# RWKV scan with partition halves holding the two scan directions of one head: 128-row products and fused score products

## The chip, the cores and the metric

The kernel runs on one core of one Trainium2 chip. The metric is the device time of one launch in microseconds (us); the change is judged by the median of several runs. Engines are named as in the profile: PE is TensorE (matrix products), PEld its weight loads, DVE is VectorE, ACT is ScalarE, POOL is GpSimd, SP is SyncE, which here only issues transfers.

## The reference

One encoder layer on a prompt of 256 tokens and a sample of 1024 tokens: feed-forward half step, token mixing, cross attention, feed-forward half step, each followed by a layer norm. Token mixing runs two groups side by side: gated linear attention, and RWKV-7 with 8 heads of 64 channels in both directions of time. The change touches only the RWKV recurrence, which the reference writes as:

```python
def _rwkv7_scan(r, decay, k, v, kk, a, reverse):
    def step(S, inp):
        r_t, w_t, k_t, v_t, kk_t, a_t = inp
        sa = jnp.einsum('bhij,bhj->bhi', S, -kk_t)
        S = (S * w_t[:, :, None, :] + sa[..., None] * (kk_t * a_t)[:, :, None, :]
             + v_t[..., None] * k_t[:, :, None, :])
        y = jnp.einsum('bhij,bhj->bhi', S, r_t)
        return S, y
...
y = (_rwkv7_scan(rH, dec_f, k2, vH, kk, aH, reverse=False)
     + _rwkv7_scan(rH, dec_b, k2, vH, kk, aH, reverse=True))
```

All of it is float32. The kernel does it in chunks of C = 64 tokens: 20 chunks (4 of the prompt, 16 of the sample), each in both directions, so a chunk step works on 8 heads x 2 directions = 16 little problems of 64x64 matrices.

## The kernel before

The program is a row of phases with all engines meeting between them. `rwkv_scan_phase` (L1202) is the one that changes; it is written out in full for each chunk, with no loop on the chip, so every product is its own instructions.

Its work is a software pipeline in four stages, `steps` calls `step(n, m, p, s)` for 23 values of n, with m = n+1, p = n+2, s = n+3:

- s: `exponentials` on ACT (L1637, L1638: `rws_grown`, `rws_decayed`) turn the loaded log decays (`rws_pack`) into factors, then `scale` on POOL (L1313 to L1322) multiplies them into `rws_bk` (the terms b and k), `rws_ar` (the terms a and r) and `rws_carry`.
- p: `scores` on PE multiply `bk` by `ar`; DVE masks the results (`mask_with`, L1721) into `rws_gb` and `rws_gk`; `rows` on PE transpose `bk` through an identity and ACT copies that out (L1673).
- m: a triangular system is inverted by doubling, in five levels: `lower`, a mask on DVE (`mask_lower`, L1715, `rws_y`), `extend`, and the copies `take_x` (L1656) and `take_z` (L1666) on ACT.
- n: the state. `rhs_of_v`, `rhs_of_h` and `solve` give `rws_u` (copied by ACT at L1650, once a chunk), `h_of_v` and `h_of_u` the next state, `out_of_h`, `out_of_v`, `out_of_u` the output; DVE adds (L1726, L1736, L1745).

In this layout a partition half `own(e)` (rows 0 to 63 or 64 to 127) holds head e of a pair of heads; direction d and pair q lie along the free axis. Every PE product is one call of `product` (L1343) over 64 rows into 64 columns. Products that alternate e stand in the two halves of the array, and most loops interleave two kinds of product that use different quarters, such as `lower` with `h_of_u`.

Each engine takes its instructions strictly in the order of the text of `step`; semaphores join them. Two waits matter below: `pe.wait_ge(bk_set, ...)` and `pe.wait_ge(ar_set, ...)` hold the first scores of chunk p until POOL has scaled it, and `exponentials` stands at a fixed place in ACT's order.

SP loads, for each chunk, two transfers of `pack` (L1302) and two of `v` (L1303).

Of the kernel before, what the change touches and what calls it, by code (L numbers as in the profile page):

```python
# [20 lines left out]
P = 128  # L21
# [1180 lines left out]
def rwkv_scan_phase(nc, pack_d, out, consts):  # L1202
# [8 lines left out]

    with ExitStack() as ctx:
        m_ = Memory(nc, ctx, "rws")
        slots = lambda name, shape, count: [m_.sb(f"{name}{u}", shape) for u in range(count)]
        BOTH, PAIR, EDGED = [P, 2, 4, C], [P, 2, 4, 2, C], [P, 2, 4, C + 1]
        pack, v = slots("pack", [P, 2, 4, PACK - R_COL], 2), slots("v", BOTH, 4)
        decayed, grown, carry = m_.sb("decayed", EDGED), slots("grown", EDGED, 2), slots("carry", [P, 2, 4, 1], 3)
        ar, bk = slots("ar", PAIR, 4), slots("bk", PAIR, 2)  # L1230
        gb, gk = slots("gb", PAIR, 3), slots("gk", PAIR, 3)
        b_rows, k_rows = slots("b_rows", BOTH, 2), slots("k_rows", BOTH, 2)
        first, w0 = m_.sb("first", BOTH), m_.sb("w0", BOTH)
        x, z, y = m_.sb("x", BOTH), slots("z", BOTH, 2), m_.sb("y", BOTH)
        rhs, u = m_.sb("rhs", BOTH), m_.sb("u", BOTH)
        h, h_sum = slots("h", BOTH, 2), m_.sb("h_sum", BOTH)
        ps = m_.psum()
        bank = lambda i: ps[:, i * BANK:(i + 1) * BANK]
        AT_X, AT_Y, AT_U, AT_H, AT_O = 0, 2, 3, 4, 5
        AT_Z = (1, 7)  # L1240
        AT_GB, AT_GK, AT_ROWS = (6, 4), (5, 6), 6
        as_both = lambda ap: ap.rearrange("p (d q t) -> p d q t", d=2, t=C)
        each_q = lambda ap: ap.unsqueeze(2).broadcast_to(BOTH)
        col = lambda d, q: slice((4 * d + q) * C, (4 * d + q + 1) * C)
        HEAD_LANES = (slice(0, C), slice(C, P))
        own, other = (lambda e: HEAD_LANES[e]), (lambda e: HEAD_LANES[1 - e])
        DIRS = range(2)
        TILES = [(d, q) for d in DIRS for q in range(4)]
        stack_ident = consts["twice_ident"][:, 0:C]
        all_ident = stack_ident.unsqueeze(1).unsqueeze(1).broadcast_to(BOTH)  # L1250
        level_mask = lambda l: each_q(consts["level"][:, 2 * l * C:2 * (l + 1) * C].rearrange("p (d t) -> p d t", t=C))
        first_mask = each_q(consts["first"].rearrange("p (d t) -> p d t", t=C))
        within_mask = lambda d: consts["within"][:, 2 * d * C:2 * (d + 1) * C].unsqueeze(1).broadcast_to([P, 4, 2 * C])

        loaded = [m_.sem(f"loaded{u}") for u in range(2)]
        exps, bk_set, ar_set, carried = (m_.sem(n) for n in ("exps", "bk_set", "ar_set", "carried"))
        with_b, with_k, masked_b, masked_k = (m_.sem(n) for n in ("with_b", "with_k", "masked_b", "masked_k"))
        b_turned, k_turned, b_rows_set, k_rows_set = (m_.sem(n) for n in ("b_turned", "k_turned", "b_rows_set", "k_rows_set"))
        first_set, w0_set, x_done, x_set, z1_done, z1_set, z_done, z_set = (
            m_.sem(n) for n in ("first_set", "w0_set", "x_done", "x_set", "z1_done", "z1_set", "z_done", "z_set"))  # L1260
        y_done, y_set, rhs_done, rhs_set, u_done, u_set = (m_.sem(n) for n in ("y_done", "y_set", "rhs_done", "rhs_set", "u_done", "u_set"))
        h_done, h_summed, h_set, o_done, o_added = (m_.sem(n) for n in ("h_done", "h_summed", "h_set", "o_done", "o_added"))
        zeroed = m_.sem("zeroed")
# [8 lines left out]
        def skewed(tile, width, at0, at1):  # L1272

            whole = tile[:, :, :, 0:C]
            return bass.AP(whole.tensor, whole.offset + at0, [list(whole.ap[0]), [4 * width + at1 - at0, 2], [width, 4], [1, C]])

        def skewed_edge(tile, width, at0, at1):
            whole = tile[:, :, :, 0:1]
            return bass.AP(whole.tensor, whole.offset + at0, [list(whole.ap[0]), [4 * width + at1 - at0, 2], [width, 4], [1, 1]])

        now = lambda tile: skewed(tile, C + 1, 1, 0)
        before = lambda tile: skewed(tile, C + 1, 0, 1)
        edge = lambda tile: skewed_edge(tile, C + 1, 0, C)
        packed = lambda c, at: pack[c % 2][:, :, :, at - R_COL:at - R_COL + C]
# [7 lines left out]
        @block.sync  # L1292
        def _(sp):
            for c in range(N_CHUNKS):
                if c >= 2:
                    sp.wait_ge(exps, 2 * (c - 1))
                    sp.wait_ge(bk_set, 2 * (c - 1))
                    sp.wait_ge(ar_set, 2 * (c - 1))
                if c >= 4:
                    sp.wait_ge(o_done, c - 3)  # L1300
                for d in DIRS:
                    sp.dma_start(pack[c % 2][:, d], pack_d[chunk_of(c)[d]][:, :, R_COL:PACK]).then_inc(loaded[c % 2], 16)  # L1302
                    sp.dma_start(v[c % 4][:, d], pack_d[chunk_of(c)[d]][:, :, V_COL:V_COL + C]).then_inc(loaded[c % 2], 16)  # L1303

        @block.gpsimd
        def _(pool):
            def scale(c):
                pool.wait_ge(loaded[c % 2], 64 * (c // 2 + 1))
                pool.wait_ge(exps, 2 * (c + 1))
                if c >= 2:  # L1310
                    pool.wait_ge(b_turned, c - 1)
                    pool.wait_ge(k_turned, c - 1)
# [6 lines left out]
                if c >= 1:  # L1319
                    if c >= 4:  # L1320
                        pool.wait_ge(h_set, c - 2)
# [19 lines left out]
        def _(pe):  # L1341
# [111 lines left out]
            def step(n, m, p, s):  # L1453
                state, inverting, preparing = n is not None, m is not None, p is not None

                if inverting:
                    wait_lower(m, 1)
# [758 lines left out]
```

## Time and profile before

| what | us |
|---|---|
| runs, median (3 runs, 4268.45 to 4277.95) | 4269.61 |
| profiled execution, device time | 4273.0 |
| its span in the trace | 4271.2 |
| scan: first load issued to last output product, 1848.4 to 2438.8 | 590.4 |
| mean granted clock of TensorE over the span, share of full speed | 0.936 |

The profile has a page for the whole span (busy time of each engine, the span in 40 slices, costliest groups) and views that can be asked of a stretch: busy time of each engine in windows, who waited for whom, and the instructions in order of time. The scan is one seventh of the span, so the page's totals say little of it; the windows and the timelines of that stretch do. A float32 product leaves two records of weights (PEld) and two of products (PE).

### The profile page before, as it was taken

The numbers are of one execution on the slowest core, as the hardware profiler recorded it, in microseconds if no ns is written. First come the engines' busy times: TensorE is split into PE (matmuls) and PEld (weight loads), VectorE is DVE, ScalarE is ACT, GpSimd is POOL, SyncE is SP. The second block draws the span as 40 slices with busy tenths as digits, with TensorE's granted clock in tenths as the row PEclk, the third lists the DMA queues.
The fourth block names the chain that finished last, engine by engine and source line by source line (L and its number), as shares of the span: only waits on it lengthen the run. The fifth ranks groups of instructions, "written<-read, shape, count | busy, mean of one in ns | idle before, by whom it ended". The sixth has DMA issues, their size and how long they took to land. (4 is left out here: it accounts for less than half of the span.)

```text
span 4271.2 us, 79008 instructions
## 1 busy us (share of the span) xinstructions
PE 3590.2 (84%) x34136; PEld 3040.9 (71%) x34136; DVE 1767.0 (41%) x2278; ACT 967.7 (23%) x1223; POOL 326.9 (8%) x302
## 2 busy tenths in 40 slices
PE   7999999996999465646667758977896999999997
PEld 6888888875888363346666636866785888888885
DVE  4444544445000476732323242240316444544445
ACT  2111111103111345523333332131304111111112
POOL 0000000001000151022222010010001000000000
PEclk9999999998999777779999979988998999999998
DMA  2101011002222202841222123001000101101001
GB/s 104 44 29 44 34 40 44 29 5 80 84 82 83 92 1 97 208 137 57 73 73 59 67 72 140 25 25 45 20 27 33 45 29 44 41 33 44 29 20 50
DMA packets 107410, 244.64 MB, mean 57 GB/s; under 512 B 26176, under 2 KB 72512, under 8 KB 100800
## 3 DMA queue, kind: packets, MB, share of 16 engines
q1 hardware_dynamic: 101008, 219.56, 15.5%
q10 hardware_dynamic: 6192, 21.89, 1.3%
q8 instruction: 179, 2.93, 0.3%
q14 instruction: 31, 0.25, 0.0%
HBM read 185.38 MB, written 56.05 MB: 57 GB/s over the span
## 5 line engine op out<-in xcount | busy, mean ns | idle before, releaser
L292 DVE TENSOR_TENSOR main_acc<-main_acc,ffn_psum 128x512 f32<-128x512 f32 (+1 forms) x1056 | 617.3, 598 | 853.5 <-PE ffn_psum L215 852.8
L204 PE MATMUL ffn_psum<-x_xh,ffn_wi_h 128*128 128x512 f32 (+1 forms) x2112 | 525.3, 357 | 52.8 <-DVE ffn_wi_l L281 52.8
L204 PE MATMUL ffn_psum<-x_xl,ffn_wi_h 128*128 128x512 f32 (+1 forms) x2112 | 525.2, 357 | 0.0
L204 PE MATMUL ffn_psum<-x_xh,ffn_wi_l 128*128 128x512 f32 (+1 forms) x2112 | 525.1, 357 | 0.0
L204 PEld LDWEIGHTS ffn_psum<-x_xh,ffn_wi_h 128*128 128x128 f32 x2112 | 372.6, 188 | 120.7 <-DVE ffn_wi_l L281 53.2
L204 PEld LDWEIGHTS ffn_psum<-x_xl,ffn_wi_h 128*128 128x128 f32 x2112 | 349.6, 188 | 61.2
L204 PEld LDWEIGHTS ffn_psum<-x_xh,ffn_wi_l 128*128 128x128 f32 x2112 | 349.9, 188 | 60.6
L215 PE MATMUL ffn_psum<-ffn_hid_h,ffn_wo_h 128*128 128x512 f32 (+1 forms) x1056 | 380.5, 360 | 12.6 <-DVE ffn_hid_l L300 10.0
L215 PE MATMUL ffn_psum<-ffn_hid_h,ffn_wo_l 128*128 128x512 f32 (+1 forms) x1056 | 377.7, 358 | 0.0
L215 PE MATMUL ffn_psum<-ffn_hid_l,ffn_wo_h 128*128 128x512 f32 (+1 forms) x1056 | 376.5, 357 | 0.0
L256 ACT CAST ffn_hid_h<-ffn_hid 128x1280 fp32r<-128x1280 f32 x44 | 55.7, 1267 | 1090.6 <-DVE ffn_hid L298 1090.6
L215 PEld LDWEIGHTS ffn_psum<-ffn_hid_h,ffn_wo_h 128*128 128x128 f32 x1056 | 198.9, 188 | 62.6 <-DVE main_acc L292 12.0
L215 PEld LDWEIGHTS ffn_psum<-ffn_hid_h,ffn_wo_l 128*128 128x128 f32 x1056 | 198.9, 188 | 31.5
L215 PEld LDWEIGHTS ffn_psum<-ffn_hid_l,ffn_wo_h 128*128 128x128 f32 x1056 | 199.4, 189 | 16.6
L1715 DVE TENSOR_TENSOR rws_y<-rws_psum,mix_consts 128x512 f32<-128x512 f32 x100 | 69.2, 692 | 314.8 <-PE rws_psum L1343 314.4
L376 PE MATMUL mixin_psum<-x_xh,mixin_w_h 128*128 128x512 f32 (+1 forms) x648 | 162.7, 359 | 19.9 <-DVE mixin_w_l L418 19.9
L418 DVE TENSOR_TENSOR mixin_w_l<-mixin_w_raw,mixin_w_h 128x1024 fp32r<-128x1024 f32 x27 | 33.0, 1225 | 330.1 <-ACT mixin_w_h L386 330.1
L1343 PE MATMUL rws_psum<-rws_x,rws_gb 64*64 64x64 f32 x3200 | 131.0, 228 | 43.6 <-issue 40.8
L564 POOL TENSOR_TENSOR x_xl<-main_acc,x_xh 128x2048 fp32r<-128x2048 f32 x12 | 54.2, 4514 | 1476.3 <-ACT x_xh L553 1476.3
L252 ACT ACTIVATE ffn_hid<-ffn_psum 128x1280 f32<-128x1280 f32 x44 | 54.7, 1242 | 494.7 <-PE ffn_psum L204 494.7
L376 PE MATMUL mixin_psum<-x_xl,mixin_w_h 128*128 128x512 f32 (+1 forms) x648 | 162.4, 359 | 0.0
L376 PE MATMUL mixin_psum<-x_xh,mixin_w_l 128*128 128x512 f32 (+1 forms) x648 | 162.3, 359 | 0.0
(304 smaller groups left out, 5800.9 us busy)
## 6 DMA issues: line engine op xcount, KB each, us to landing
ffn_w_raw_in<-ffn_w_in_dram SPq DMA_DIRECT2D x44, 1024.0 KB, 5.5
rws_pack<-pack SPq DMA_DIRECT2D x40, 772.0 KB, 5.6
ffn_w_raw_out<-ffn_w_out_dram SPq DMA_DIRECT2D x44, 512.0 KB, 3.6
proj<-mixin_stage ACTq DMA_DIRECT2D x27, 640.0 KB, 3.0
mixin_w_raw<-mix_w_in_dram SPq DMA_DIRECT2D x27, 512.0 KB, 3.5
pack<-rwp_pack SPq DMA_DIRECT2D x4, 2580.0 KB, 11.3
rwp_raw<-proj SPq DMA_DIRECT2D x15, 640.0 KB, 8.5
kv_w_raw<-ca_w_kv_dram SPq DMA_DIRECT2D x16, 512.0 KB, 3.5
```

What stands on the lines that cost most here:

```text
L204: mm = nc.tensor.matmul(ps[:, at + c * BANK:at + c * BANK + tn], w[:, slot, cols], x[:, k, t0:t0 + tn], start=(k == 0 and j == 0), stop=(k ...
L215: mm = nc.tensor.matmul(ps[:, at:at + tn], w[:, slot, o * P:(o + 1) * P], h[:, t0:t0 + tn], start=(j == 0), stop=(j == 2))
L252: nc.scalar.activation(hid[:], ps[:, gate_at:gate_at + T], ACT.Silu).then_inc(silu_done, 1)
L256: nc.scalar.copy(hid_h[:], hid[:]).then_inc(hid_high, 1)
L292: nc.vector.tensor_tensor(acc[:, o, t0:t0 + tn], acc[:, o, t0:t0 + tn], ps[:, at:at + tn], ALU.add).then_inc(added, 1)
L376: mm = nc.tensor.matmul(ps[:, at:at + tn], w[:, u, k * P:(k + 1) * P], x[:, k, t0:t0 + tn], start=(k == 0 and j == 0), stop=(k == KT - 1 a ...
L418: nc.vector.tensor_tensor(w_l[:, u, :], raw[:, u, :], w_h[:, u, :], ALU.subtract).then_inc(split, 1)
L564: nc.gpsimd.tensor_tensor(xl[:, :, tok(s)], acc[:, :, tok(s)], xh[:, :, tok(s)], ALU.subtract).then_inc(low, 1)
L1343: return nc.tensor.matmul(dst, lhs, rhs_, start=start, stop=stop, skip_group_check=True)
L1715: nc.vector.tensor_tensor(y[:], as_both(bank(AT_Y)), level_mask(level), ALU.mult).then_inc(y_set, 1)
```

## The change

- A partition half now holds a direction, `own(d)`; the 8 heads lie along the free axis (`HEADS`, `WIDE`). The two terms of one head (h and v, u and v, b and k, a and scores) are put in the two halves of a tile, so that a sum of two products over 64 rows becomes one product over 128 rows: `right_side` for `rhs_of_v` and `rhs_of_h`, `next_h` for `h_of_v` and `h_of_u`, `out_of_uv` for `out_of_v` and `out_of_u`.
- `scores` takes b and k together as 128 columns of weights and a, r and an identity together as 192 moving columns (`ar[:, :, 2]` holds the identity), so one product gives both score matrices and the transposed rows. There are four sets of four such products in a step, over one pair of PSUM banks; the next set waits for ACT's `take_rows` of the one before.
- DVE masks each set with three instructions (L1636 to L1638 of the new kernel) instead of one mask of 512 columns.
- ACT: `take_rows` four times 256 columns; `keep_a` copies a into `left`; `take_u` in two halves; `exponentials` now stands behind `take_z(m, 3)`.
- POOL: `scale` has one product for r over all lanes, and for a, b and k six over 64 lanes and the full 512 columns, and two small ones for `carry`. It also fills the identities once.
- SP: eight transfers of pack and eight of v a chunk; v goes into both `hv` and `uv`.
- `lower` of levels 2 to 5 and `solve` stand alone in PE's order, not interleaved with products of another kind.

```diff
-            def scores(c, term, d, at, i):
-
-                q, e = i // 2, i % 2
-                return product(bank(at)[own(e), 2 * q * C:2 * (q + 1) * C], bk[c % 2][own(e), d, q, term],
-                               ar[c % 4][own(e), d, q].rearrange("p a t -> p (a t)"))
...
+            def scores(c, n):
+
+                d, j0 = SETS[n]
+                if n == 0:
+                    pe.wait_ge(bk_set, 4 * (c + 1))
+                    pe.wait_ge(ar_set, 3 * (c + 1))
+                if n or c:
+                    pe.wait_ge(rows_set, 4 * c + n)
+                for i in range(4):
+                    pair = bk[c % 2][own(d), j0 + i].rearrange("p a t -> p (a t)")
+                    at = (AT_S + i // 2) * BANK + i % 2 * 3 * C
+                    mg = product(ps[:, at:at + 3 * C], pair, ar[c % 4][own(d), j0 + i].rearrange("p a t -> p (a t)"))
+                mg.then_inc(scored, 1)
...
+            def right_side(c, j, d):
+                return product(bank(AT_UH)[other(d), col(j)], left[c % 3][:, d, j], hv[c % 2][:, d, j])
+
+            def next_h(c, j, d):
+                return product(bank(AT_UH)[own(d), col(j)], rows[c % 3][:, d, j], uv[c % 2][:, d, j])
...
+            def out_of_uv(c, j, d):
+                at = (4 * d + j // 2) * C
+                return product(bank(AT_O)[LANES[j % 2], at:at + C], uv[c % 2][:, d, j], gr[c % 3][:, d, j], start=False)
...
-                nc.gpsimd.tensor_tensor(bk[c % 2][:, :, :, 0], packed(c, B_COL), now(grown[c % 2]), ALU.mult).then_inc(bk_set, 1)
-                nc.gpsimd.tensor_tensor(bk[c % 2][:, :, :, 1], packed(c, K_COL), now(grown[c % 2]), ALU.mult).then_inc(bk_set, 1)
...
+                for d in DIRS:
+                    nc.gpsimd.tensor_tensor(ar[c % 4][own(d), :, 0], packed(KK_AT, own(d)), decayed[own(d), :, 2 * d:2 * d + C], ALU.mult).then_inc(ar_set, 1)
...
+                for d in DIRS:
+                    for at, place in ((B_AT, d), (K_AT, 1 - d)):
+                        nc.gpsimd.tensor_tensor(bk[c % 2][own(d), :, place], packed(at, own(d)), grown[c % 2][own(d), :, 1:C + 1], ALU.mult).then_inc(bk_set, 1)
...
+                nc.vector.tensor_tensor(four(gr[c % 3][:, d, j0:j0 + 4]), score_part(slice(0, P), 1), mask(upto(d)), ALU.mult)
+                nc.vector.tensor_tensor(four(left[c % 3][other(d), d, j0:j0 + 4]), score_part(other(d), 0), mask(before(d)[other(d)]), ALU.mult)
+                nc.vector.tensor_tensor(four(gb[c % 2][own(d), j0:j0 + 4]), score_part(own(d), 0), mask(before(d)[own(d)]), ALU.mult).then_inc(masked, 1)
```

POOL's order of one step, before: the two instructions that make `rws_w` for the inversion, then `scale` of the next chunk.

```order
L1326 TENSOR_TENSOR rws_first<-rws_gb,mix_consts 128x512 [waits rws_masked_b]
L1330 TENSOR_TENSOR rws_w<-rws_first,mix_consts 128x512 [waits rws_z1_done,rws_first_set]
L1313 TENSOR_TENSOR rws_bk<-rws_pack,rws_grown 128x8x64 [waits rws_b_turned,rws_k_turned,rws_exps,rws_loaded1]
L1314 TENSOR_TENSOR rws_bk<-rws_pack,rws_grown 128x8x64
L1317 TENSOR_TENSOR rws_ar<-rws_pack,rws_decayed 128x8x64 [waits load_x_in0]
L1318 TENSOR_TENSOR rws_ar<-rws_pack,rws_decayed 128x8x64
L1322 TENSOR_TENSOR rws_carry<-rws_grown 128x8 [waits load_x_in1]
```

The same place in the changed kernel:

```order
L1337 TENSOR_TENSOR rws_w<-rws_gb,mix_consts 128x512 [waits rws_z1_done,rws_masked,rws_bk_set]
L1339 TENSOR_TENSOR rws_w<-rws_w,mix_consts 128x512 [waits rws_first_set]
L1317 TENSOR_TENSOR rws_ar<-rws_pack,rws_decayed 128x8x64 [waits rws_scored,load_x_in1,rws_exps,rws_loaded1]
L1320 TENSOR_TENSOR rws_ar<-rws_pack,rws_decayed 64x8x64 [waits rws_ar_set]
L1320 TENSOR_TENSOR rws_ar<-rws_pack,rws_decayed 64x8x64
L1326 TENSOR_TENSOR rws_carry<-rws_grown 64x8 [waits load_x_in2]
L1326 TENSOR_TENSOR rws_carry<-rws_grown 64x8
L1330 TENSOR_TENSOR rws_bk<-rws_pack,rws_grown 64x8x64 x4
```

Four wide instructions of `scale` have become seven, six of them over 64 partitions with as many elements in each partition as before.

ACT's order from the copy of u to the last copies of the inversion, before (`rws_grown` is the first of the two exponentials):

```order
L1650 COPY rws_u<-rws_psum 128x512
L1656 COPY rws_x<-rws_psum 128x512
L1666 COPY rws_z<-rws_psum 128x512
L1637 ACTIVATE rws_grown<-rws_pack 128x520
L1638 ACTIVATE rws_decayed<-rws_pack 128x520
L1673 COPY rws_b_rows<-rws_psum 128x512
L1656 COPY rws_x<-rws_psum 128x512
L1666 COPY rws_z<-rws_psum 128x512
```

And in the changed kernel:

```order
L1561 COPY rws_uv<-rws_psum 64x512 x2
L1548 COPY rws_rows<-rws_psum 128x256
L1567 COPY rws_x<-rws_psum 128x512
L1577 COPY rws_z<-rws_psum 128x512
L1548 COPY rws_rows<-rws_psum 128x256
L1541 COPY rws_left<-rws_ar 64x512 x2
L1567 COPY rws_x<-rws_psum 128x512
L1577 COPY rws_z<-rws_psum 128x512
L1533 ACTIVATE rws_grown<-rws_pack 128x528
L1534 ACTIVATE rws_decayed<-rws_pack 128x528
```

The exponentials have moved behind one more pair of copies, the fourth `take_rows` and `keep_a`.

PE's order in the changed kernel at the head of a step; these are the first scores of chunk p between the 128-row products of chunk n and the interleaved pair of `lower` and `extend_z`:

```order
L1354 MATMUL rws_psum<-rws_hv,rws_left 64x64 x15
L1354 MATMUL rws_psum<-rws_ar,rws_bk 128x192 [waits rws_rows_set,rws_ar_set,rws_bk_set]
L1354 MATMUL rws_psum<-rws_ar,rws_bk 128x192 x3
L1354 MATMUL rws_psum<-rws_x,rws_gb 64x64 [waits load_high,rws_z_set,rws_x_set]
L1354 MATMUL rws_psum<-rws_x,rws_gb 64x64
L1354 MATMUL rws_psum<-rws_z,rws_y 64x64 x2
```

In the kernel before, the place of the wait for `bk_set` and `ar_set` was the second group of a step, and scores stood there one by one between products of another kind:

```order
L1343 MATMUL rws_psum<-rws_v,rws_gk 64x64
L1343 MATMUL rws_psum<-rws_ar,rws_bk 64x128
L1343 MATMUL rws_psum<-rws_v,rws_gk 64x64 x2
L1343 MATMUL rws_psum<-rws_ar,rws_bk 64x128
```

The wait has moved from behind 32 products to behind 16, and all scores of a set now stand in one block. Over the whole scan PE has 7040 products instead of 8960.

## Rows read from the trace of the kernel before

**Rows 1.** Busy time by window: us, each engine's busy time (records), clock, DMA share, GB/s
```profile
1848.40:1862.90 14.50, 0.01 (x2) 0.04 (x2) 4.81 (x2) 1.24 (x3) 4.59 (x4) 0.50 0.83 254
1862.90:1902.80 39.90, 32.00 (x1134) 30.18 (x1137) 11.95 (x18) 13.38 (x25) 15.65 (x15) 0.93 0.32 96
...
1902.80:2390.00 487.20, 335.88 (x15233) 318.58 (x15225) 145.95 (x222) 160.52 (x289) 131.57 (x120) 0.96 0.22 65
```

**Rows 2.** The copy of u, once a chunk: count, durations, first and last start
```profile
L1650 ACT COPY rws_u<-rws_psum x20: 587/587/589, 1902.8 to 2434.2; 128x512 f32<-128x512 f32 x20
```

**Rows 3.** Waits within the scan, 1895 to 2400 us: total, times, longest
```profile
PE rws_psum L1343 <- issue: 155.3, 117, 3.5
```

**Rows 4.** Windows from one gap of PE to the next, the scan's own instructions
```profile
2109.95:2113.65 3.70, 2.75 (x126) 2.62 (x127) 1.28 (x2) 0.59 (x1) 1.00 0.02 4
...
2121.10:2125.95 4.85, 2.82 (x127) 2.57 (x126) 0.69 (x1) 1.76 (x3) 1.00 1.06 346
```

**Rows 5.** DMA queues, 2100 to 2200 us: packets, MB, share of 16 engines
```profile
q8 instruction: 24, 0.39, 1.7%
```

**Rows 6.** PE in order of time: start, us, operation, count, idle before
```profile
2108.05 0.86 PE L1343 MATMUL rws_psum<-rws_v,rws_k_rows 64*64 64x64 f32 x23
2110.00 0.45 PE L1343 MATMUL rws_psum<-rws_v,rws_k_rows 64*64 64x64 f32 x8 [1.09 <-issue]
2110.25 0.27 PE L1343 MATMUL rws_psum<-rws_x,rws_gb 64*64 64x64 f32 x2
...
2110.68 0.25 PE L1343 MATMUL rws_psum<-rws_x,rws_gb 64*64 64x64 f32 x2
```

**Rows 7.** The scan's line by form: shortest, median and longest ns
```profile
L1343 PE MATMUL rws_psum<-rws_ar,rws_bk x1280: 266/269/472, 1862.9 to 2389.9; 64*64 64x128 f32 x183
...
L1343 PE MATMUL rws_psum<-mix_consts,rws_bk x1280: 212/218/267, 1870.1 to 2404.4; 64*64 64x64 f32 x183
```

**Rows 8.** PE in order of time in the GLA scan, products with 128 weight columns
```profile
1583.04 0.39 PE L837 MATMUL glas_psum<-glas_qs_pair,glas_state 128*128 128x128 f32 x2
1583.27 0.39 PE L836 MATMUL glas_psum<-glas_s_pair,glas_v_rows 128*128 128x128 f32 x2
```

**Rows 9.** POOL in order of time, one step of the scan
```profile
2110.46 1.20 POOL L1313 TENSOR_TENSOR rws_bk<-rws_pack,rws_grown 128x512 f32<-128x512 f32 x1 [2.35 <-ACT rws_decayed L1638]
2111.61 1.19 POOL L1314 TENSOR_TENSOR rws_bk<-rws_pack,rws_grown 128x512 f32<-128x512 f32 x1
...
2113.89 1.64 POOL L1318 TENSOR_TENSOR rws_ar<-rws_pack,rws_decayed 128x512 f32<-128x512 f32 x1
2115.49 0.20 POOL L1322 TENSOR_TENSOR rws_carry<-rws_grown 128x8 f32<-128x8 f32 x1
```

**Rows 10.** Groups by form, smaller operands: busy us, mean ns, idle before
```profile
L780 POOL TENSOR_TENSOR glas_ko_pair<-gla_k_out,mix_consts 128x256 f32<-128x256 f32 x40 | 29.1, 727 | 0.0
...
L1745 DVE TENSOR_TENSOR main_acc<-main_acc,rws_psum 128x256 f32<-128x256 f32 x40 | 15.0, 418 | 13.6 <-PE rws_psum L1343 13.6
...
L856 ACT COPY glas_k_pair<-gla_k_in 64x128 f32 x72 | 21.4, 298 | 2.2 <-PE glas_psum L812 0.4
L861 ACT COPY glas_v_rows<-glas_psum 128x256 f32<-128x256 f32 x40 | 15.3, 383 | 49.3 <-PE glas_psum L803 49.3
```

**Rows 11.** ACT in order of time, one step of the scan
```profile
2108.66 0.59 ACT L1666 COPY rws_z<-rws_psum 128x512 f32<-128x512 f32 x1
2109.14 0.66 ACT L1637 ACTIVATE rws_grown<-rws_pack 128x520 f32<-128x520 f32 x1
2109.69 0.64 ACT L1638 ACTIVATE rws_decayed<-rws_pack 128x520 f32<-128x520 f32 x1
```

**Rows 12.** DVE in order of time, same step
```profile
2105.56 0.69 DVE L1715 TENSOR_TENSOR rws_y<-rws_psum,mix_consts 128x512 f32<-128x512 f32 x1 [0.15 <-PE rws_psum L1343]
...
2112.81 1.68 DVE L1736 TENSOR_TENSOR rws_h<-rws_h_sum,rws_carry 128x512 f32<-128x512 f32 x1
```

**Rows 13.** SP's issues in order of time
```profile
2147.12 0.63 SPq L1303 DMA_DIRECT2D rws_v<-pack  x1
```

More of the change, by code:

```diff
@@ L1250, in rwkv_scan_phase @@
[L1250 to L1256, printed above, removed]
@@ new lines, in rwkv_scan_phase @@
+        heads = lambda ap: ap.rearrange("p (j t) -> p j t", t=C)
+        each_head = lambda ap, n=8: ap.unsqueeze(1).broadcast_to([ap.shape[0], n, ap.shape[1]])
+        col = lambda j: slice(j * C, (j + 1) * C)
+        LANES = (slice(0, C), slice(C, P))
+        own, other = (lambda d: LANES[d]), (lambda d: LANES[1 - d])
+        DIRS = range(2)
+        TILES = [(j, d) for j in range(8) for d in DIRS]
+        ident = consts["twice_ident"][:, 0:C]
+        level_mask = lambda l: each_head(consts["level"][:, l * C:(l + 1) * C])
@@ new lines, in rwkv_scan_phase @@
+        first_mask = each_head(consts["first"])
+        before = lambda d: consts["within"][:, 2 * d * C:(2 * d + 1) * C]
+        upto = lambda d: consts["within"][:, (2 * d + 1) * C:(2 * d + 2) * C]
+        SETS = [(0, 0), (1, 0), (0, 4), (1, 4)]
+        loaded, v_loaded = [m_.sem(f"loaded{u}") for u in range(2)], [m_.sem(f"v_loaded{u}") for u in range(2)]
+        ready, exps, bk_set, ar_set, carried, a_kept = (m_.sem(n) for n in ("ready", "exps", "bk_set", "ar_set", "carried", "a_kept"))
@@ L1381, in rows @@
-            def rows(c, term, i):
-                d, q = TILES[i]
-                for e in range(2):
-                    mm = product(bank(AT_ROWS)[own(e), col(d, q)], bk[c % 2][own(e), d, q, term], stack_ident[own(e)])
-                return mm
-            def rhs_of_v(c, i):
-                d, q = TILES[i]
-                for e in range(2):
-                    mm = product(bank(AT_U)[other(e), col(d, q)], gk[c % 3][own(e), d, q, 0], v[c % 4][own(e), d, q], start=(i == 0), stop=False)
-                return mm
@@ L1688, in step @@
                     take_z(m, 2)
-                if s is not None:
-                    exponentials(s)
                 if p is not None:
-                    take_rows(p, 0)
+                    take_rows(p, 3)
+                    keep_a(p)
                 if m is not None:
@@ L2136, in constant_table @@
              "within": np.concatenate([before[0], upto[0], before[1], upto[1]], 1),
-             "first": np.concatenate([levels[1], levels[0]], 1), "level": np.concatenate(levels, 1)}
+             "first": np.where(row < C, levels[1], levels[0]),
+             "level": np.concatenate([np.where(row < C, levels[2 * n + 1], levels[2 * n]) for n in range(LEVELS)], 1)}
     return {n: v.astype(np.float32) for n, v in parts.items()}
```

482 lines of the change are left out of this document (205 added, 277 removed).

## The prediction, on record before the changed kernel ran

> **What bounds the kernel now.** I read the windows first. The scan runs from 1848.4 to 2438.8 us, 590 of 4271 us: 14.5 us from the first load to the first scores, 39.9 us to fill the pipeline [rows 1], and from then on one copy of u a chunk [rows 2]: 17 intervals in 487.2 us, 28.7 us each, and two last ones, with nothing left to prepare, in 44.2 us. In the 487 us PE is busy for 336 us, ACT 161, DVE 146, POOL 132: no engine is full, and the clock stands at 0.96, nearly always its 2.4 GHz level. Next come the waits. PE's idle time in the scan is put down to "issue" alone, 155 us in 117 pieces [rows 3], and the windows from one such gap to the next hold 253 records each, weights and products together [rows 4]. In the same stretch the queue of instructions brings 24 packets in 100 us, 0.39 MB [rows 5]: 16 KB each, and one packet for each such window. So PE runs through straight code faster than the code is brought. A block costs 3.70 us, and 4.85 us where the chunk's loads run at the same time [rows 4]; a step has 448 products of four records, 1792 records, seven blocks of some 255: 7 x 3.7 = 26 us and some 2.5 us for the block under the loads and other waits, which is the 28.7 us measured. The number of PE instructions is the price of a step now.
>
> **What the change takes from PE.** 7040 products instead of 8960 are 352 instead of 448 a step, 1408 records, 5.5 blocks: 5.5 x 3.75 = 20.6 us, and with the same 2.5 us 23 us. If code were still the bound, a step would lose 5.5 us.
>
> **What PE itself then needs.** A stream in two quarters of the array passes 23 records in 0.86 - 0.22 us, 28 ns each, 56 ns a product [rows 6]; with all four quarters in use, 28 records from 2110.25 to 2110.68, 15 ns each [rows 6]. The new score product has 128 weight columns and 192 moving ones over 64 rows. From 64 to 128 moving columns a record grows from 218 to 269 ns [rows 7], so 51 ns per 64 columns; 192 columns occupy the array for about 0.16 us a record, 0.32 us a product. Records with 128 columns of weights and of data follow at 0.11 us [rows 8], so the wider weights hide under 0.16. Four products of a set sit in one row half and cannot share the array: 1.3 us a set, 5.2 us a step. The other 336 products stand in 14 groups, of 16 in two quarters or 32 in four, 0.9 us each, and two half groups: 13.5 us. The sum is 18 to 19 us of array time: not a bound by itself. The 128-row products are in no row; I take two of them, in the two column halves, as running side by side like two 64-row ones (0.9 us for 16), with 1.8 us as the other end.
>
> **What the change puts between the sets of scores.** Here the order matters. A set's scores go to one pair of banks, DVE masks them in three instructions, ACT takes the rows, and only then may PE write the next set. Prices: a DVE instruction of 256 columns takes 0.42 us [rows 10]; a queued instruction starts before the last one ends (ACT's are 0.59 long and 0.48 apart, [rows 11]), so I take 0.34 between starts, an estimate; the 64-partition ones I price by columns, because on ACT a copy of 64 partitions and 128 columns takes 0.298 us against 0.383 for 128 partitions and 256 columns [rows 10], so partitions save nothing. Three of them: 1.1 us. `take_rows` 0.39 us. The last product's result leaves 0.2 us after it starts [rows 7], and two hand-overs cost 0.1 each and more on PE, 0.25 in all. One turn is 1.3 + 0.2 + 1.1 + 0.39 + 0.25 = 3.25 us. PE has other work in it: 0.9 us between sets 0 and 1, so it waits there.
>
> **The loop.** I follow it from the first scores of chunk p to the first of chunk p+1.
> - Set 0 to set 1: 3.25 us.
> - Set 1 to set 2: on ACT the copy of x now stands behind `take_rows`, and `lower` of level 2 needs x. 3.0 to the end of `take_rows`, x 0.59 [rows 11], hand-over 0.2, `lower` 0.9, half of `out_of_h` 0.45, a change of array shape 0.2: 5.3 us.
> - Set 2 to set 3: 3.25 us.
> - Set 3 to the end of `extend` of level 3: 1.3 + 0.2 + 1.1, mask of y 0.69 [rows 12], hand-over 0.2, `extend` 0.9 and its result 0.2: 4.6 us.
> - ACT: x and z 1.1, then the exponentials 0.55 + 0.64 [rows 11]: 2.3 us with the hand-over.
> - POOL: `scale` has seven wide instructions. One follows another after 1.15 us [rows 9]; the narrower 128x256 one takes 0.73 [rows 10]. Six of the seven have 64 partitions and the full 512 elements in each. If an instruction costs by its elements in a partition, that is 7 x 1.15 + 2 x 0.2 + 0.3 of hand-overs = 8.8 us; if by elements in all, 1.15 + 6 x 0.73 + 0.7 = 6.2 us. I take the first, since the ACT row above behaves so, and keep the second as a rival.
> The sum is 3.25 + 5.3 + 3.25 + 4.6 + 2.3 + 8.8 = 27.5 us. Before, the exponentials stood in front of this chain's second half (2109.14, [rows 11]), POOL ended at 2115.7 [rows 9], 6.6 us later, and its results were wanted only at the head of the next step (steps are 28.7 us long): slack, which the change spends. The first scores wait for `bk_set` and `ar_set` at PE's head, and behind them on PE stands everything: `lower`, `solve`, the state. Copies and `extend` of levels 4 and 5 are done in the meantime, and PE idles some 4 us a step there instead of in short gaps.
>
> To 27.5 us I add 1.5 us. A block that is brought late still delays a link of the chain, above all under the loads (4.85 against 3.70 [rows 4]); one POOL instruction in a step took 1.64 us while DVE's only product of two SBUF operands ran [rows 9, 12]; and the granted clock may fall to its 1.2 GHz level after the longer idle stretch, as it stood at 0.50 before the first scores [rows 1]. Bounds: nothing (27.0 us, without a cost for the shape changes either) and 4 us (128-row products one after another, +1; the rest at twice my price). So 29.0 us a step.
>
> The Trainium skill, page "TensorEngine Tiling (Array Packing)", section Tiling Modes, says that changing the tiling mode drains TensorE. The scan before never leaves 64x64, so no row shows it. By that rule the twelve changes of shape a step would each pay about one product's length: 0.2 us each, of which five lie on the loop, 1 us against the 0.2 that I have named. The range has room for it.
>
> **Loads.** Sixteen transfers a chunk instead of four, at 0.63 us of issue each [rows 13], are 10 us of SP a step of 28, and their buffers are free a step ahead; nothing waits for them but the first chunk. They load less pack and v twice; I leave the block under the loads as it is.
>
> **Head, fill and tail.** Head: first chunk's loads are issued in 8 x 0.63 instead of 4 x 0.63 us, +2.5, and POOL has three more wide instructions, +3.5: +6 us. The identities and memsets lie under the load. Fill: with chunk 0 alone a step is three turns, then 2.6 to the last mask, `take_rows` 0.4, `keep_a` 1.1, exponentials 1.2, POOL 8.8: 24 us; the next, with one inversion, 27; from there to the first u 7 us. 58 against 39.9 [rows 1]: +18 us. Tail: fewer instructions in two steps that are bound by code: -3 us.
>
> **Sum.** 17 x (29.0 - 28.7) = +6, head +6, fill +18, tail -3: +27 us. The profiled execution took 4273.0 us and its span 4271.2, the median is 4269.6; the difference goes on the median: 4297 us, slower by 0.6%.
>
> **Rivals.**
> - *The loop at my price* (0.55): 28.2 to 30 us a step, 4283 to 4314 us.
> - *POOL's 64-partition instructions at 0.73 us* (0.20, other side): six in each step save 2.5 us, so 26.5 us a step, -37; the fill saves 7.5. 4270 + 6 + 18 - 7.5 - 3 - 37 = 4246 us. For it: fewer elements. It decides from about 1 us an instruction, where the steps win back the fill. Against it: the ACT row; and if it holds, code and PE's waits at 25 us stop the gain soon. The Trainium skill, page "GPSIMD Engine Reference", says that core k works on its own 16 partitions; by that rule 64 partitions only leave half the cores idle, the price stays 1.15 and this rival falls. No row here shows it.
> - *The chain as short as my lower bounds* (0.12): 27.0 to 27.9 us a step; the steps gain 13 to 28 us and pay just for fill and head: 4262 to 4278 us.
> - *PE loses more* (0.13): shape changes drain at each place, 128-row products don't overlap, and the clock halves after the wait for POOL. 30 to 33 us a step, 4314 to 4364 us.
> - *Code stays the bound*, 23 us a step: 4195 us. Only if POOL and the score turns cost half of the rows; inside the 0.20, under 0.03.
>
> **Numbers.** Slower by over 0.2%, which is about what a measurement of this kernel tells from no change (8.5 us): 0.55 + 0.13 = 0.68. Same 0.12. Faster 0.20. The range takes in the POOL rival's time and half of the last: 4240 to 4345 us.
>
> **What would show it.** Right: u's copies 28 to 30 us apart; `rws_ar` and `rws_bk` on POOL 1.15 to 1.2 us each also with 64 partitions; PE idle until POOL's `rws_bk`, 3 to 5 us a step; gaps put down to issue well under 155 us. Wrong: a POOL instruction of 64 partitions under 1 us, PE still idle for issue alone, scores of one set overlapping (pitch under 0.1 us a record), or first u copied less than 50 us after the first scores. If the 128-row products start 0.11 us apart, not 0.056, the step is longer by 1 us and more.

## The result and the profile after

The changed kernel takes 4371.85 us (median of 4 runs, 4370.35 to 4374.56) against 4270.85 us (median of 4 runs, 4268.45 to 4277.95): the ratio is 1.0234, with a 95% interval from 1.0217 to 1.0252. It is 101 us slower; 27 were forecast. The profiled span is 4370.3 us against 4271.2, the mean granted clock 0.91 against 0.936.

Where the 99 us between the spans lie is read from the windows of the scan: first load to first scores, to the first copy of u, to the 18th, to the 20th. The columns are us, busy time with records of PE, PEld, DVE, ACT and POOL, granted clock, DMA share and GB/s.

```profile
1847.30:1867.20 19.90, 0.00 (x1) 0.04 (x1) 5.29 (x3) 1.18 (x2) 11.09 (x15) 0.50 0.75 132
1867.20:1941.45 74.25, 52.46 (x826) 46.22 (x828) 16.29 (x36) 16.70 (x34) 22.78 (x22) 0.56 0.37 67
1941.45:2492.35 550.90, 457.17 (x11972) 416.01 (x11969) 204.41 (x391) 193.49 (x375) 194.33 (x187) 0.82 0.28 55
2492.35:2532.50 40.15, 33.84 (x1209) 31.11 (x1207) 15.86 (x27) 14.92 (x28) 2.54 (x2) 0.99 0.08 17
```

| stretch | before, us | after, us | forecast of the difference | measured |
|---|---|---|---|---|
| head | 14.5 | 19.9 | +6 | +5.4 |
| fill | 39.9 | 74.25 | +18 | +34.4 |
| 17 intervals of u | 487.2 | 550.9 | +6 | +63.7 |
| two last intervals | 44.2 | 40.15 | -3 | -4.0 |

The two middle lines carry all of the miss, and they are also the lines in which the clock column has changed: 0.93 before against 0.56 in the fill, 0.96 against 0.82 in the intervals [rows 1]. The engine's clock has the two levels 1.2 and 2.4 GHz, so a share of 0.82 over 550.9 us is 2 x 0.18 x 550.9 = 198 us at the low one; before, 2 x 0.04 x 487.2 = 39 us. In the tail, at 0.99, there is nothing of this, and the forecast of that line holds.

What PE waits for from 1950 to 2400 us (total us, times, longest) is what was forecast. The wait for issue, 137 us in the same 450 us of the kernel before (the first line), is gone (the others):

```profile
PE rws_psum L1343 <- issue: 137.2, 103, 3.5
...
PE rws_psum L1354 <- POOL rws_bk L1330: 54.7, 14, 4.0
PE rws_psum L1354 <- ACT rws_x L1567: 18.8, 28, 0.7
PE rws_psum L1354 <- ACT rws_rows L1548: 3.5, 14, 0.2
PE rws_psum L1354 <- issue: 0.2, 1, 0.2
```

The queue of instructions brings 18 packets in 100 us (2200 to 2300 us) where it brought 24 [rows 5]:

```profile
q8 instruction: 18, 0.29, 1.3%
```

One step shows how the wait and the clock hang together. PE in order of time (start, us, operation, count, idle before), the five sets of scores from one step's first to the next one's:

```profile
2221.60 2.92 PE L1354 MATMUL rws_psum<-rws_ar,rws_bk 64*128 64x192 f32 x8 [3.47 <-POOL rws_bk L1330]
...
2226.37 2.92 PE L1354 MATMUL rws_psum<-rws_ar,rws_bk 64*128 64x192 f32 x8
...
2234.52 1.56 PE L1354 MATMUL rws_psum<-rws_ar,rws_bk 64*128 64x192 f32 x8
...
2237.87 1.56 PE L1354 MATMUL rws_psum<-rws_ar,rws_bk 64*128 64x192 f32 x8 [0.25 <-ACT rws_rows L1548]
...
2254.51 2.92 PE L1354 MATMUL rws_psum<-rws_ar,rws_bk 64*128 64x192 f32 x8 [3.94 <-POOL rws_bk L1330]
```

The same eight records take 2.92 us behind the wait and 1.56 us later in the step: the two levels of the clock. The windows of this step say so directly:

```profile
2221.50:2224.00 2.50, 2.40 (x7) 2.40 (x8) 0.00 (x0) 0.00 (x0) 0.05 (x1) 0.50 0.36 70
2224.00:2233.00 9.00, 9.00 (x176) 8.01 (x177) 3.13 (x7) 2.46 (x6) 0.00 (x0) 0.50 0.60 130
2233.00:2246.00 13.00, 12.08 (x363) 11.02 (x364) 7.80 (x14) 6.21 (x12) 3.41 (x3) 0.98 0.02 4
2246.00:2254.50 8.50, 3.89 (x180) 3.55 (x170) 1.12 (x3) 2.73 (x5) 8.00 (x9) 0.96 0.35 64
```

PE is idle for 3.47 us, and then it works for 11.4 us at 1.2 GHz without a pause: 183 records of products, where the following 13 us take 363. The step shown, 32.9 us from first scores to first scores, is the longer of two that alternate; the next one takes 31.9. The last line is the link that makes PE idle: POOL busy for 8.00 of 8.50 us. There, POOL in order of time:

```profile
2245.14 1.08 POOL L1317 TENSOR_TENSOR rws_ar<-rws_pack,rws_decayed 128x512 f32<-128x512 f32 x1 [1.71 <-ACT rws_decayed L1534]
2246.30 2.42 POOL L1320 TENSOR_TENSOR rws_ar<-rws_pack,rws_decayed 64x512 f32<-64x512 f32 x2
2248.80 0.49 POOL L1326 TENSOR_TENSOR rws_carry<-rws_grown 64x8 f32<-64x8 f32 x2
2249.36 5.09 POOL L1330 TENSOR_TENSOR rws_bk<-rws_pack,rws_grown 64x512 f32<-64x512 f32 x4
```

And its instructions by form (busy us, mean ns, idle before), the 64-partition ones above the 128-partition one:

```profile
L1330 POOL TENSOR_TENSOR rws_bk<-rws_pack,rws_grown 64x512 f32<-64x512 f32 x80 | 100.1, 1271 | 3.0
L1320 POOL TENSOR_TENSOR rws_ar<-rws_pack,rws_decayed 64x512 f32<-64x512 f32 x40 | 47.1, 1176 | 3.1
...
L1317 POOL TENSOR_TENSOR rws_ar<-rws_pack,rws_decayed 128x512 f32<-128x512 f32 x20 | 22.0, 1098 | 40.3 <-ACT rws_decayed L1534 35.4 <-issue 4.9
```

### The profile page after: what moved, and what is told of

It reads as the page before. It is cut to its first block and busy times, and to the rows that moved or that the text cites. A ratio compares the mean times of both kernels' runs of the same rounds, so it can differ in the third digit from the quotient of the medians.

```text
span 4370.3 us, 71906 instructions
## 1 busy us (share of the span) xinstructions
PE 3733.2 (85%) x30296; PEld 3151.9 (72%) x30296; DVE 1835.5 (42%) x2478; ACT 1004.6 (23%) x1323; POOL 401.6 (9%) x389
## 5 line engine op out<-in xcount | busy, mean ns | idle before, releaser
L1354 PE MATMUL rws_psum<-rws_ar,rws_bk 64*128 64x192 f32 x640 | 181.3, 443 | 118.3 <-POOL rws_bk L1330 108.0
L1354 PEld LDWEIGHTS rws_psum<-rws_ar,rws_bk 64*128 64x128 f32 x640 | 148.8, 259 | 129.3 <-POOL rws_bk L1330 77.0
```

The lines of the kernel that those rows point to most:

```text
L1354: return nc.tensor.matmul(dst, lhs, rhs_, start=start, stop=stop, skip_group_check=True)
```

## The experiments

My theory after this reading: the loop through POOL is as long as forecast, PE's idle stretch at its end brings the clock down for a third of the step, and a fill in which PE waits in every turn stays at the low level. The rival: the new products and the changes of array shape themselves cost more than priced, and the clock only goes with them. "Step" below is the mean of the 17 intervals from the first copy of u to the 18th: 28.7 us before, 32.4 us after. Times are medians, with the ratio to the kernel before and its 95% interval.

### Keep PE at work during the wait

16 products of two constant tiles, into columns of the score banks that nothing reads, stand where PE waits for POOL. Nothing else of the changed kernel is touched.

```diff
                     mr.then_inc(rhs_done, 1)
+                if state and preparing:
+                    for i in range(16):
+                        product(ps[:, (AT_S + i % 2) * BANK + 6 * C:(AT_S + i % 2 + 1) * BANK], consts["head_ones"], consts["ones"])
                 if preparing:
                     scores(p, 0)
```

> The changed kernel with 16 products of 128x128 float32 constants (0.22 us each, 3.5 us) put between right_side and the wait for POOL, into 128 unused columns of the score banks; the output is unchanged. My theory: the step's loop through POOL is 28 to 28.5 us at the 2.4 GHz level, and the other 3.7 us of the 32.2 us that a step takes are products run at the 1.2 GHz level after PE's 3.9 us of idling. So the products keep the clock up and the time falls by 17 x 3.7 = 63 us, to 4290 to 4320 us, mean clock of the scan over 0.93. Rival: the chain of masks, copies and POOL is itself 3 us longer than I summed, and the low clock costs nothing on it: 4372 to 4400 us, no faster, since PE only has more to do.

Measured: 4312.67 us (4305.22 to 4313.88), 1.009 [1.0072, 1.0108]; a step is 28.7 us. More work made the kernel 59 us faster. The window from 1950 to 2400 us, of the kernel before and of the changed kernel, then of this one:

```profile
1950.00:2400.00 450.00, 311.93 (x14098) 295.96 (x14098) 135.67 (x205) 148.43 (x267) 118.86 (x107) 0.96 0.21 62
1950.00:2400.00 450.00, 372.68 (x9787) 339.26 (x9784) 166.39 (x318) 157.87 (x306) 159.16 (x154) 0.82 0.30 60
```

```profile
1950.00:2400.00 450.00, 408.83 (x11536) 372.94 (x11535) 187.54 (x361) 173.88 (x345) 183.21 (x176) 1.00 0.33 66
```

The clock is 1.00, and PE waits for POOL's `rws_bk` for almost nothing, since the constant products fill the wait:

```profile
PE rws_psum L1354 <- ACT rws_x L1570: 23.8, 46, 0.7
PE rws_psum L1354 <- ACT rws_rows L1551: 14.2, 30, 0.7
PE rws_psum L1354 <- POOL rws_bk L1330: 2.2, 10, 0.2
```

This run also gives each link of the loop without the clock. Its four sets of scores in one step (PE in order of time):

```profile
2224.46 1.56 PE L1354 MATMUL rws_psum<-rws_ar,rws_bk 64*128 64x192 f32 x8 [0.20 <-POOL rws_bk L1330]
...
2227.81 1.56 PE L1354 MATMUL rws_psum<-rws_ar,rws_bk 64*128 64x192 f32 x8 [0.70 <-ACT rws_rows L1551]
...
2233.14 1.56 PE L1354 MATMUL rws_psum<-rws_ar,rws_bk 64*128 64x192 f32 x8
...
2236.49 1.56 PE L1354 MATMUL rws_psum<-rws_ar,rws_bk 64*128 64x192 f32 x8 [0.25 <-ACT rws_rows L1551]
```

POOL's first product of the next chunk starts at 2243.76 us; in the step ahead it started at 2215.05, and PE's scores 9.4 us later, at 2224.46. For the changed kernel the same differences come from the five rows of scores and POOL's start at 2245.14:

| link of the loop | forecast | changed kernel | with PE kept at work |
|---|---|---|---|
| set 0 to set 1 | 3.25 | 4.77 | 3.35 |
| set 1 to set 2 | 5.3 | 8.15 | 5.33 |
| set 2 to set 3 | 3.25 | 3.35 | 3.35 |
| set 3 to POOL's first product | 6.9 | 7.27 | 7.27 |
| POOL to the next set 0 | 8.8 | 9.37 | 9.4 |
| sum | 27.5 | 32.9 | 28.7 |

Only the two links behind the wait differ between the last two columns, by 1.42 and 2.82 us, 4.2 us in this step. In the shorter one of the two that alternate they differ by 1.4 and 1.8, 3.2 us, so 3.7 us in the mean. That is the clock; the rival falls, since every product of the changed kernel is there in both, in the same order and shape.

### The exponentials earlier on ACT

```diff
                 if p is not None:
                     take_rows(p, 0)
+                if s is not None:
+                    exponentials(s)
...
                     take_x(m, 3)
                     take_z(m, 3)
-                if s is not None:
-                    exponentials(s)
```

> The changed kernel with the exponentials back near the head of ACT's step (behind the first take_rows), nothing else. POOL still makes rws_w first, and that needs the last masks of the step. My theory: POOL starts scale some 1.7 us earlier, bound now by rws_w; the idle stretch of PE shrinks from 3.9 to about 2.2 us and with it some of the time at the low clock: 30 us a step, 4372 - 17 x 2.2 = 4335 us (4310 to 4345). Rival, the exponentials are not on the loop: 4372 us.

Measured: 4304.37 us (4302.87 to 4313.76), 1.0082 [1.0063, 1.0101]; a step is 28.5 us. The gain is 67 us where 37 were expected, and the time lies below the expected range. The wait for POOL and the window of the same stretch:

```profile
PE rws_psum L1354 <- POOL rws_bk L1330: 35.8, 16, 2.3
```

```profile
1950.00:2400.00 450.00, 368.30 (x11129) 332.41 (x11129) 198.82 (x363) 175.66 (x348) 192.24 (x175) 0.96 0.33 66
```

PE still idles in each step, for 2.2 us instead of 3.9, but the clock is back at 0.96. Eleven of the 17 steps are 26.9 to 27.8 us at a granted clock of 1.00; the other six are 29.8 to 31.2, at 0.84 to 0.89. So the loop itself became shorter by 1.0 us (28.7 to 27.7), and the rest of the 3.9 us a step is the clock again.

Why 1.0 and not the 2.3 us of ACT's link? POOL had been waiting for the exponentials for no more than 1.71 us (the row of L1317 above): the rest of them was hidden behind POOL's own work for `rws_w`, which I had left out of the chain. From set 3 to POOL's first product it is now 5.5 us instead of 7.27, but from there to the next set 0 it is 10.2 instead of 9.4. POOL's products, now earlier, coincide with DVE's product of two SBUF operands, and both take longer: this one 1.53 us where it took 1.08, and DVE's pair 2.39 where it took 1.61.

```profile
2091.27 2.39 DVE L1655 TENSOR_TENSOR rws_hv<-rws_hv,rws_carry 64x512 f32<-64x512 f32 x2
2091.57 1.53 POOL L1317 TENSOR_TENSOR rws_ar<-rws_pack,rws_decayed 128x512 f32<-128x512 f32 x1
```

### POOL's work for the next chunk ahead of its work for this one

In addition to the edit above, `scale` now stands ahead of `first_level` in POOL's step, so that the score turns no longer lead into POOL.

```diff
             def step(n, m, p, s):
-                if p is not None:
-                    first_level(p)
                 if s is not None:
                     scale(s)
+                if p is not None:
+                    first_level(p)
```

> As e_exp_early, and POOL does scale of the next chunk before it makes rws_w, so that POOL is off the loop. My theory: the loop through POOL is gone, PE no longer idles at the head of a step, the clock stays up, and a step costs what the turns of the four score sets, and code at 5.5 blocks of 3.75 us, leave: 24.5 to 26 us, so 4372 - 17 x 6.9 = 4255 us (4235 to 4275), faster than both kernels. Rival, the score turns of mask and copy are the bound and POOL only stood behind them: 30 us a step or more, above 4320 us.

Measured: 4233.34 us (4231.79 to 4233.93), 0.991 [0.9893, 0.9926]; a step is 24.7 us. That is just below the expected range. It beats the kernel before by 38 us and the changed one by 138 us. POOL in order of time, one step, and what PE waits for from 1950 to 2400 us:

```profile
2202.76 1.09 POOL L1317 TENSOR_TENSOR rws_ar<-rws_pack,rws_decayed 128x512 f32<-128x512 f32 x1 [11.71 <-ACT rws_decayed L1534]
...
2207.03 5.11 POOL L1330 TENSOR_TENSOR rws_bk<-rws_pack,rws_grown 64x512 f32<-64x512 f32 x4
2213.13 1.29 POOL L1337 TENSOR_TENSOR rws_w<-rws_gb,mix_consts 128x512 f32<-128x512 f32 x1 [1.00 <-POOL rws_bk L1330]
```

```profile
PE rws_psum L1354 <- ACT rws_x L1567: 27.1, 51, 0.7
PE rws_psum L1354 <- ACT rws_rows L1548: 14.9, 31, 0.7
...
PE rws_psum L1354 <- issue: 0.9, 3, 0.4
```

POOL does the same work in the same time, 2202.76 to 2212.14 us, but it is done 10.7 us before PE's next first scores (2222.83 us), and 11.71 us of POOL's idle time now lie ahead of it. No wait for `rws_bk` is left, and the granted clock of the window is 1.00. With PE busy for 401 of 450 us here, against 312 before, and no wait above 0.9 us within the scan, the step is now mostly PE's own. So the new layout is worth 4 us a step (28.7 to 24.7), 68 us over the 17, once POOL is off the loop. It takes both edits: in the changed kernel `scale` starts when the exponentials end, 1.71 us after the work for `rws_w`, so that order alone, which was not run, would by these rows move nothing; the exponentials alone gave 67 of the 138 us.

### Constant products in the fill

On top of the last kernel, constant products ahead of the sets of scores of the first two chunks, into the output bank before anything is accumulated there.

```diff
                 d, j0 = SETS[n]
+                if c < 2:
+                    for i in range(24 if c + n == 0 else 8):
+                        product(bank(AT_O)[:, 0:P], consts["head_ones"], consts["ones"])
```

> e_pool_free with constant products (128x128 float32) in the first two steps only: 24 before the first scores and 8 before each later set of chunks 0 and 1, into the bank of the output, which is not in use yet. Output unchanged. My theory: the fill runs at the 1.2 GHz level because PE is idle before and between the sets (first u 74 us after the first scores in the changed kernel, 58 forecast); kept busy, it runs at 2.4 GHz and the fill loses 10 to 14 us: 4233 - 12 = 4221 us (4216 to 4227). Rival, the fill is set by DVE, ACT and POOL and the products only add to it: 4233 to 4245 us.

Measured: 4227.37 us (4223.59 to 4233.45), 0.9909 [0.9892, 0.9925]. The windows of the fill, without and with them:

```profile
1867.00:1900.00 33.00, 23.17 (x208) 19.87 (x208) 8.03 (x19) 6.73 (x15) 15.13 (x15) 0.50 0.62 113
1900.00:1931.00 31.00, 26.77 (x516) 24.13 (x516) 7.09 (x14) 9.73 (x19) 8.21 (x9) 0.59 0.23 45
```

```profile
1867.00:1900.00 33.00, 27.89 (x304) 25.23 (x305) 7.93 (x19) 7.68 (x16) 15.28 (x16) 0.80 0.63 113
1900.00:1931.00 31.00, 27.07 (x760) 24.46 (x760) 10.12 (x21) 11.09 (x22) 13.98 (x14) 1.00 0.23 46
```

The clock of the fill did rise, and the first copy of u came 6.5 us earlier (1927.0 against 1933.5 us), about half of what was expected. The added products stand in the way themselves (304 records instead of 208 in the first window). The medians differ by 6 us with overlapping ranges: of the 16 us by which the fill was mis-sized this shows some 6 to be the clock's. The rest is read from the fill's own steps, below.

### Is PE's instruction stream the bound of the kernel before?

Four edits of the kernel before. First, more instructions with almost no work: 64 products of one column in each full step, 256 records, which is one block of code.

```diff
+                if state and preparing:
+                    for i in range(64):
+                        product(bank(AT_Y)[other(i % 2), 0:1], stack_ident[own(i % 2)], stack_ident[own(i % 2), 0:1])
```

> The kernel before, with 64 products of one moving column (256 more instructions, one more block of code) in each full step, 17 of them, into columns that are overwritten; the output is unchanged. Code as the bound says: one block more a step, +3.7 us x 17 = +63 us, 4333 us (4320 to 4345). A bound by dependencies between engines says less than +20 us, since PE has 9 us of idle time a step.

Measured: 4360.97 us (4360.71 to 4363.81), 1.0208 [1.0191, 1.0225]; a step is 33.7 us, 5.0 more, where 3.7 were expected, and the time lies above the expected range of 4320 to 4345 us. That is more than one block of code costs [rows 4], and the window shows why it can't be read as code alone:

```profile
1950.00:2400.00 450.00, 351.33 (x13547) 340.77 (x13540) 111.90 (x173) 124.85 (x225) 100.79 (x91) 0.85 0.21 61
```

The clock is 0.85 instead of 0.96, though PE is busy for 351 us instead of 312. The experiment agrees in sign and settles no size.

Second, more work in the same instructions: 128 moving columns instead of 64 in 28 of the 32 products that transpose rows.

```diff
-                    mm = product(bank(AT_ROWS)[own(e), col(d, q)], bk[c % 2][own(e), d, q, term], stack_ident[own(e)])
+                    at = (4 * d + q) * C
+                    wide = 2 * C if i < 7 else C
+                    mm = product(bank(AT_ROWS)[own(e), at:at + wide], bk[c % 2][own(e), d, q, term], consts["twice_ident"][own(e), 0:wide])
```

> The kernel before, with 128 moving columns instead of 64 in 28 of the 32 transposing products of a step; what they write too much is overwritten. No instruction more, 28 x 2 records x 51 ns over two quarters of the array, 1.4 us of PE time a step. If code is the bound, this is free: 4271 us, within 5 us. If PE's own time or the chain between the engines is the bound: up to +1.4 x 20 = +28 us, 4295 us.

Measured: 4271.83 us (10 runs, 4267.1 to 4279.69) against 4269.41, 1.0008 [0.9998, 1.0017]. PE is busy for 1.8 us more in each step, and the step is as long as before (28.7 us): work in the array costs nothing measurable there.

Third, fewer instructions: `out_of_v` and `out_of_u` are left out, 32 of 448 products, so the output lacks these two terms.

```diff
                     for i in range(8):
-                        out_of_h(n, i)
+                        mo = out_of_h(n, i)
...
-                    if state:
-                        out_of_v(n, i)
...
-                    for i in range(8):
-                        mo = out_of_u(n, i)
```

> The kernel before without out_of_v and out_of_u, so the output lacks these two of its three terms in every chunk: 128 of 1792 instructions a step fewer, half a block of code. No other engine waits for more or less than before but DVE's last add. If code is the bound: -1.85 us x 20 = -37 us, 4234 us (4225 to 4245). If the chain between the engines is the bound: within 10 us of before, since these products stand beside it.

Measured: 4228.78 us (4227.49 to 4229.7), 0.991 [0.9893, 0.9926]; a step is 26.4 us, 2.2 less. 128 records of 1792 are half a block, 0.5 x 3.7 = 1.85 us by [rows 4], and PE's busy time fell by only 1.2 us a step. Together the last two say that the kernel before paid for the number of PE's instructions and not for their columns. They stand at different places of the step, so that a part of the 2.2 us could still be the place of the products left out.

Fourth, the slack of POOL that the forecast said was spent: the exponentials behind `take_z(m, 3)`, as in the changed kernel, and three more wide products of POOL, into tiles that nothing reads.

```diff
+                nc.gpsimd.tensor_tensor(spare[0][:], packed(c, B_COL), now(grown[c % 2]), ALU.mult)
+                nc.gpsimd.tensor_tensor(spare[1][:], packed(c, B_COL), now(grown[c % 2]), ALU.mult)
+                nc.gpsimd.tensor_tensor(spare[2][:], packed(c, B_COL), now(grown[c % 2]), ALU.mult)
```

> The kernel before, with POOL as late and as long as in the changed one: the exponentials behind take_z(m, 3), and three more wide instructions of scale into tiles that nobody reads. My theory: before, POOL's results wait about 10 us for the head of the next step, so its later end (exponentials +5 us, instructions +3.5 us) is just covered: 4271 to 4290 us. Rival, the late POOL alone makes the loss, with no help from the score turns: 4330 us or more.

Measured: 4277.04 us (10 runs, 4271.25 to 4286.26) against 4269.41, 1.0021 [1.0012, 1.0031], and the first copy of u is 10.7 us later (1913.4 us) while the steps stay at 28.6. A lateness that costs the changed kernel its gain costs the old layout nothing in the steps. The timelines say why: before, POOL ended 11 us ahead of PE's next first scores (2115.7 and 2126.7 us), and here, with 9 us more, it still ends 4 us ahead of them. What the changed kernel adds is its four score turns: POOL's first product of the next chunk starts there only 23.5 us after the first scores (2245.14 and 2221.60 us).

## Why the prediction was right and wrong

**The bound before** was read right: wider instructions are free, and fewer save time. **The new bound** was named right too, with its place (the first scores of a chunk), its length of wait (3.5 to 3.9 us where "some 4 us" stood) and the late exponentials in it; that POOL makes `rws_w` ahead of `scale` is not in its chain. The waits for issue went from 137 us to 0.2 in 450.

**Prices.** Without the low clock the links of the loop came out at 28.7 us against 27.5: the three links between sets are right within 0.1 us each, ACT's and DVE's link is 0.4 long, POOL's 0.6. Instructions with 64 partitions cost POOL 1.18 to 1.27 us, as much as one with 128 (1.10), so the rival in which they take 0.73 falls. The rule that the Trainium skill gives on the page "GPSIMD Engine Reference" (Extended-addressing connectivity: for `tensor_tensor` each core works on its own 16 partitions) agrees with these rows. DVE and ACT do the same: 422 ns for `rws_gb` of 64 partitions against 424 for `rws_gr` of 128, and 580 for `rws_uv` of 64x512 against 587 of 128x512 [rows 2].

```profile
L1636 DVE TENSOR_TENSOR rws_gr<-rws_psum,mix_consts 128x256 f32<-128x256 f32 x80 | 33.9, 424 | 288.3 <-PE rws_psum L1354 288.3
L1638 DVE TENSOR_TENSOR rws_gb<-rws_psum,mix_consts 64x256 f32<-64x256 f32 x80 | 33.8, 422 | 1.1
```

The 128-row products do run side by side in the two column halves: 17 records in 0.74 us, (0.74 - 0.22) / 16 = 0.033 us apart, so 0.065 us for a product of two records. The forecast took 0.056 and had 0.11 as its other end.

```profile
2217.39 0.74 PE L1354 MATMUL rws_psum<-rws_hv,rws_left 128*64 128x64 f32 x17 [0.24 <-issue]
```

**The step that failed** is the one that adds 1.5 us to 27.5. It listed three causes, a late block, POOL's slow instruction and the clock "after the longer idle stretch", and gave them 1.5 us together with 4 us as the upper bound. The links without the clock use up 1.2 of it (28.7 - 27.5), and late blocks nothing. The clock alone then costs 32.4 - 28.7 = 3.7 us in the mean step. This is the term that was mis-sized: I had priced it as a thing that may happen. It happened in every step, for 198 / 17 = 11.7 us in the mean, because the loop has the idle stretch in every turn and PE's two links behind it (set 0 to 1, set 1 to 2) are made of PE's own work, which takes nearly twice as long at 1.2 GHz. The material for this stood in the windows ahead of the prediction: the head's clock of 0.50 [rows 1], and 1.3 us a set of scores which I never doubled. 3.7 x 17 = 63 us are lost to it. The run with the constant products got them back in the steps, and 59 in all, since its first copy of u came 3.8 us later.

The page "TensorE: Matmul & The Clock Gate" of the Trainium skill (HAM oscillation) tells of a kernel in which TensorE, left waiting for a transfer before each tile of work, fell to the low clock and began every tile there. This case's rows agree, with POOL in the transfer's place; taken up as a rival it would have given the low clock to the first two links of each step and to the fill.

**The fill** failed for the same reason. With only one or two chunks in the pipeline PE waits in every turn, and the clock is 0.50 from the first scores to 1928 us. The first scores of chunks 0, 1 and 2, with the second set of chunk 0, and the window:

```profile
1867.20 2.90 PE L1354 MATMUL rws_psum<-rws_ar,rws_bk 64*128 64x192 f32 x8 [33.73 <-POOL rws_bk L1330]
1871.96 2.93 PE L1354 MATMUL rws_psum<-rws_ar,rws_bk 64*128 64x192 f32 x8 [1.87 <-ACT rws_rows L1548]
...
1897.70 2.92 PE L1354 MATMUL rws_psum<-rws_ar,rws_bk 64*128 64x192 f32 x8 [7.48 <-POOL rws_bk L1330]
...
1934.05 1.56 PE L1354 MATMUL rws_psum<-rws_ar,rws_bk 64*128 64x192 f32 x8 [0.47 <-POOL rws_bk L1330]
```

```profile
1867.20:1928.00 60.80, 40.68 (x512) 35.41 (x512) 12.54 (x28) 12.20 (x25) 17.08 (x16) 0.50 0.35 62
```

The two steps of the fill take 30.5 and 36.4 us where 24 and 27 stood, and from there to the first copy of u it is 7.4 where 7 stood. So the 16 us lie in the two steps at the low level: 6.5 and 9.4. The second of them is 7.7 us longer than a whole step of the run with constant products (28.7 us, clock 1.00), though it has less for PE to do. In the first, the three turns between sets are 4.6 to 4.8 us each, 1.4 more than forecast, 4.3 in all. By this some 12 of the 16 us are the clock's, an estimate from one trace; the run made for it recovered 6.5 us, with its own products in the way.

**The range** ended at 4345 us. The rival "PE loses more" had the right mechanism in it (the clock halves after the wait for POOL), but it went to 33 us a step and kept the fill at 58 us; 32.4 us a step with the fill at 74 us lies beyond it. The two terms have one cause, so their upper ends belonged together. **Head and tail** came out as worked out, +5.4 and -4.0 for +6 and -3.

**Changes of array shape** were cheap. Behind a group of the same shape the first record starts 0.2 us before the last one ends, behind another shape 0.07 before (2234.52 + 1.56 = 2236.08 against a start at 2236.01 in the changed kernel): 0.15 us each, nearer the 0.2 us that the prediction put on a change than nothing, and not a bound.

## What to carry to other kernels

When a change cuts the instructions of the engine that bounds the kernel, follow the next-longest loop round all engines and ask whether it leaves that engine idle once a turn. If it does, price TensorE's work behind the wait at both levels of the clock, and put a pipeline's fill, where it waits in every turn, at the low one. And look at the order of independent blocks on the helper engines first: here the exponentials early in ACT's step and, on POOL, the next chunk's `scale` ahead of this chunk's `first_level`, both together, turned a loss of 101 us into a gain of 38.

## What the runs showed of the hardware

- Filling an idle stretch with useless products paid: 16 constant products a step, 59 us less in all, by the clock alone (0.82 to 1.00).
- After an idle stretch of 3.5 to 3.9 us, PE ran at 1.2 GHz for 11.4 us of unbroken work in the step shown, 11.7 us in the mean step. With the exponentials earlier the stretches were 2.3 us at most, and over 450 us the clock was 0.96, as before the change: 1.00 in eleven of 17 steps, and 0.84 to 0.89 in six.
- With 64 products of one column more in each step of the kernel before, the clock was 0.85 instead of 0.96 although PE was busy for 351 us of 450 instead of 312. With 16 constant ones of full width in the changed kernel it was 1.00. Why is open: kernel, width and place of the products all differ.
- Where a product on POOL and one on DVE, both with all operands in SBUF, coincided, both took longer: 1.53 us instead of 1.08 on POOL and 2.39 instead of 1.61 on DVE. Before, one on POOL took 1.64 us beside one on DVE [rows 9, 12].
- Half of the partitions saved no time on POOL (1.18 to 1.27 us against 1.10), DVE (422 ns against 424) or ACT (580 against 587), while it doubles the number of instructions.
